# A hybrid attention layer on one core: the inverse softmax sums are turned on VectorE before they are stored

## What is computed

```python
p = softmax(s)                      # per query and head: exp(s - max) / sum
o = einsum(p, v)                    # A, B and M alike; B adds exp(sink - max) to the sum
y = concat([o_a, o_b, o_m], -1) * silu(gate)
x = x + einsum('btm,md->btd', y, w_out)
```

## Time and profile before

| | |
|---|---|
| median of three runs | 1607.84 us |
| lowest and highest | 1602.36, 1608.74 us |
| the profiled execution's own time | 1599.02 us |
| its span, first to last instruction | 1597.2 us |
| PE busy | 1400.2 us, 88% of the span |
| DVE busy | 920.6 us, 58% |
| ACT busy | 657.4 us, 41% |
| POOL busy | 155.9 us, 10% |
| mean granted TensorE clock | 0.949 of full speed |

### The profile page before, as it was taken

How to read it: one execution, slowest core, us unless ns; L and a number is a source line. 1 busy time by engine, 2 the same in 40 slices (tenths; PEclk the granted TensorE clock), 3 DMA queues, 4 the chain that set the end, 5 groups by cost and what they waited for, 6 DMA issues and landing times. The chain is left out here.

```text
span 1597.2 us, 19488 instructions
## 1 busy us (share of the span) xinstructions
PE 1400.2 (88%) x6364; PEld 778.1 (49%) x6364; DVE 920.6 (58%) x2527; ACT 657.4 (41%) x1667; POOL 155.9 (10%) x187
## 2 busy tenths in 40 slices
PE   5988799999889999988599887999997999998881
PEld 3444356666545444444344343666664444544450
DVE  1444636887656677655133446488775557676533
ACT  1123526776634433333111334377655333344332
POOL 1100013300001000000011001132000001000003
PEclk9999999999989999999689998999998999999976
DMA  6100410123132312111241004003124222111106
GB/s 200 53 25 21 156 47 1 45 88 94 67 88 73 80 53 54 26 35 29 62 160 52 25 18 161 27 0 119 35 86 133 54 57 57 54 47 53 34 4 247
DMA packets 117960, 108.58 MB, mean 68 GB/s; under 512 B 52368, under 2 KB 90992, under 8 KB 117872
## 3 DMA queue, kind: packets, MB, share of 16 engines
q1 hardware_dynamic: 117872, 107.45, 22.1%
HBM read 81.76 MB, written 25.76 MB: 67 GB/s over the span
## 5 line engine op out<-in xcount | busy, mean ns | idle before, releaser
L746 PE MATMUL score_ps<-w_slot,hT 128*128 128x512 f32 (+2 forms) x1024 | 391.9, 542 | 12.5 <-ACT prob_bm L1053 7.6
L746 PEld LDWEIGHTS score_ps<-w_slot,hT 128*128 128x128 f32 x1024 | 197.7, 196 | 193.3 <-issue 187.3
L746 PE MATMUL score_ps<-w_slot,work 128*128 128x512 f32 x512 | 234.6, 612 | 5.5 <-issue 5.4
L1099 ACT ACTIVATE hT<-hT,neg_top 128x128 f32<-128x128 f32 (+8 forms) x144 | 116.8, 812 | 288.0 <-DVE neg_top L1372 287.8
L1253 DVE TENSOR_SCALAR_CACHE_REDUCE work<-bias,trial 128x384 f32<-128x384 f32 (+3 forms) x256 | 226.1, 883 | 6.9
L969 ACT ACTIVATE work<-bias,neg_trial 128x768 bf16<-128x768 f32 (+2 forms) x192 | 198.4, 1043 | 67.3 <-DVE neg_trial L1249 67.3
L746 PEld LDWEIGHTS score_ps<-w_slot,work 128*128 128x128 f32 x512 | 97.5, 196 | 129.8 <-issue 129.6
L817 PE MATMUL score_ps<-hT,w_slot 128*128 128x352 f32 x448 | 135.2, 460 | 1.4 <-ACT gate_raw L1083 1.4
L731 PE MATMUL turn_ps<-ident,hT 128*128 128x128 f32 (+1 forms) x720 | 98.9, 277 | 27.6 <-ACT work L1124 17.2
L1154 POOL TENSOR_TENSOR work<-work,norm_sb 128x512 f32<-128x512 f32 (+1 forms) x32 | 38.9, 1216 | 855.7 <-DMA norm_sb<-norm_scratch 855.7
L871 PE MATMUL score_ps<-akT,query_mem 64*128 64x512 f32 (+4 forms) x448 | 103.1, 547 | 9.4 <-ACT prob_bm L1113 6.5
(11 more groups left out here) (179 smaller groups left out, 1768.2 us busy)
## 6 DMA issues: line engine op xcount, KB each, us to landing
w_slot<-in_w_in_dram SPq DMA_DIRECT2D x8, 2048.0 KB, 10.3
gate_raw<-in_x_prompt_dram SPq DMA_DIRECT2D x16, 512.0 KB, 3.7
work<-gate_scratch SPq DMA_DIRECT2D x16, 512.0 KB, 4.7
x_scratch<-gate_raw SPq DMA_DIRECT2D x16, 512.0 KB, 4.6
gate_raw<-x_scratch SPq DMA_DIRECT2D x16, 512.0 KB, 3.5
norm_sb<-norm_scratch SPq DMA_DIRECT2D x56, 128.0 KB, 4.1
gate_scratch<-gate_raw SPq DMA_DIRECT2D x16, 264.0 KB, 3.1
gate_scratch<-gate_raw SPq DMA_DIRECT2D x8, 528.0 KB, 2.6
```

What stands on the lines that cost most here:

```text
L746: last = nc.tensor.matmul(out[:, 0:cols], lhs(k), w[:, k, 0:cols], start=(k == 0), stop=(k == KD - 1))
L1099: ins = nc.scalar.activation(p, p, ACT.Exp, bias=neg, scale=SM_SCALE, accum_out=sums[t % 2][0:r, col:col + 1])
```

## The change

`inv_sum` becomes 32 columns wide, with columns 16 to 31 zeroed once at the start of the program. SCALE makes DVE wait for its reciprocal (`link`), then transposes the tile's `inv_sum` in blocks of 32 by 32 into a new buffer `inv_turned`, of which there is one for each of a and bm and for each of two tiles. In that buffer the eight inverse sums of 32 queries lie on eight partitions, 32 elements each, one such block for every 32 partitions. DVE waits for the transposition too (`signal`), which now gives `inv_made`. `norm_turn` issues four DMAs where it issued one (one for the tile of 32 queries), each of eight rows of 128 bytes. The loads, GATE_SCALE and MIX are the same; the counts that wait for `norm_written` follow the new number of DMAs.

```diff
+def norm_writes(t):
+    return sum(-(-ROWS[n] // 32) for n in range(1, t + 1))
...
-        inv_sum = [sb(f"inv_sum{b}", [P, 16]) for b in range(2)]
+        inv_sum = [sb(f"inv_sum{b}", [P, 32]) for b in range(2)]
+        inv_turned = [[sb(f"inv_turned{b}_{bm}", [P, 32]) for bm in range(2)] for b in range(2)]
...
+                for b in range(2):
+                    nc.gpsimd.memset(inv_sum[b][:, :], 0.0)
...
                         sp.wait_ge(inv_made[bm], t)
-                        with nc.allow_non_contiguous_dma("a head's sums lie one to a partition"):
-                            sp.dma_start(rows.rearrange("c q -> q c"), inv_sum[t % 2][0:r, 8 * bm:8 * bm + 8]
+                        for q in range(0, r, 32):
+                            sp.dma_start(rows[:, q:q + 32], inv_turned[t % 2][bm][q + 8 * bm:q + 8 * bm + 8, :]
                                          ).then_inc(norm_written[bm], 16)
-                        sp.wait_ge(norm_written[bm], 16 * t)
+                        sp.wait_ge(norm_written[bm], 16 * norm_writes(t))
...
                             if t >= 3:
-                                dve.wait_ge(norm_written[bm], 16 * (t - 2))
+                                dve.wait_ge(norm_written[bm], 16 * norm_writes(t - 2))
                             at = slice(8 * bm, 8 * bm + 8)
-                            nc.vector.reciprocal(inv_sum[b][0:r, at], sums[b][0:r, at]).then_inc(inv_made[bm], 1)
+                            link(nc.vector.reciprocal(inv_sum[b][0:r, at], sums[b][0:r, at]))
+                            signal(nc.vector.transpose(inv_turned[b][bm][0:r, :], inv_sum[b][0:r, :]), inv_made[bm], t)
```

## The result

The changed kernel takes 1613.60 us (median of 6 runs, 1611.96 to 1615.43) against 1606.16 us for the kernel before beside it: a ratio of 1.0047, 95% interval [1.0034, 1.0060]. It is 7.4 us slower, and the interval excludes no change. The number lies in the range, but the forecast, nothing on the path, was wrong.

The account below looks back on a forecast made before the run. PE was taken to set the pace in the attention stages. With 0 gained and 0 lost the profiled execution stays at 1599.0 us, 8.8 under the runs' median of 1607.84, so the forecast was 1607, range 1598 to 1617.

Parts of the forecast that it names:

- nothing on the path: Whole kernel: no part of the change gains or loses time, median 1607 us; chance 0.80.
- The store gets shorter: SP's store of the inverse sums: 4.2 us (3.1 to 6.7) for 9.0, about 4.8 less, which nobody waits for.
- the first rival's condition: Slower by stores: four DMAs land one after another, 17.2 us; decides once the store takes 1.85 us longer; 1631, chance 0.06.
- On the path: 0: Attention stages: the shorter store, and separately the longer SCALE on DVE, were each taken to change the kernel's time by 0.
- DVE gets more to do: SCALE in attention grows by 0.35 us (0.28 to 0.55), 32 times, 11 us of DVE work, hidden behind PE.
- T: Time of one added DVE transposition in SCALE, taken as 0.22 us, between bounds of 0.15 and 0.42.
- The cover in front of ADD: DVE's idle time while PE does OUT: at least 0.40 us, 0.72 before PE moves, enough for the longer SCALE.
- the 6 to 13 given as a sign of being right: DVE's busy time would rise by 6 to 13 us if the prediction was right.
- Faster, through the memory system: Rival: single-element stores disturb other traffic or PE's clock; 0.3 us for each of 32 stores, 9.6 back: 1598, chance 0.09.
- The change touches only the attention stages, so I read those first: Opening step: only the two attention stages, 335 and 340 us, were read for what bounds the kernel.
- The sum: All parts together: 0 gained, 0 lost, the profiled execution stays at 1599.0 us.
- What would upset all of it: Something neither queue nor wait shows: a change of PE's granted clock in the attention stages; no size given.

Follow-up runs that it names:

- layer0_straddles: The kernel before with 30 small VectorE instructions more at the start of layer 0, nothing turned: 1620.09 us, 1.0075 times before.
- before_shift: The kernel before with 16 small VectorE instructions more at the start of layer 1, nothing turned: 1617.27 us, 1.0060 times before.

## Why the prediction was wrong

- *The store gets shorter.* Right, and mis-sized: 2.22 us with the issue where 4.2 were taken (3.1 to 6.7), and 28.1 us of SP's standing where some 90 were. The four DMAs neither wait for each other nor land as slowly as single elements do, so the first rival's condition never held.
- *On the path: 0* for the store. Right: MIX and ADD are released by PE as before, and the two kernels with turned stores and the loop elsewhere stand at 1.0008 and 1.0001.
- *DVE gets more to do.* Right: T was taken as 0.22 us and is 0.21 (32 in all, 6.7 us); SCALE grew by 0.36. The cover in front of ADD swallowed it: ADD's waits for PE fell from 118.1 to 106.4 us. VectorE's busy time rose by 17.3 us, above the 6 to 13 given as a sign of being right; 8.0 of them lie in layer 1's search.
- *Faster, through the memory system.* Not seen: packets under 512 B fell by more than half (52368 to 24017), and the kernels with turned stores and the loop elsewhere are not faster than before.
- **The failed step** is in the first sentence: "The change touches only the attention stages, so I read those first". It touches VectorE's program, which holds a loop behind the added instructions. The sum priced what the 32 transpositions do and not that 16 of them stand ahead of layer 1's loop and move it. The missing term is what this set off: 30 ways back of 0.14 us more, which PE's slack would have taken, and the meeting with GpSimd's rope, in all 7.4 us. That the measured time still lies in the range is luck: the range was made from the spread of the runs, not from this.
- *What would upset all of it*, something that neither queue nor wait shows, was also not it: the waits show it, in the row of `trial` behind `bit`, in a stage that I had not listed. That row of before would have given the warning: VectorE waits there for itself, 60 times, 23.2 us, in a stage in which PE had 1.0 of 76.9 us open.

What stays open: why the way back costs 0.51 to 0.63 us at these places, whether the change has a part in the falls of the clock at tiles 7 and 8, and the part of the total of layer0_straddles that its searches do not hold.

## What to carry to other kernels

Instructions added to an engine move all that follows in its program: when a change adds some ahead of a loop, compare the gap in front of the loop's first instruction, before and after, in every loop of that engine, and move the loop by a few idle instructions before blaming the change. A slack is to be read against what runs beside it: twice 0.14 us fitted into the 0.52 us that a pair of steps had, and still 7 us were lost, because the shift brought small instructions under another engine's long ones, and the phase then held itself. A chain that is hidden by 1.8 us is worth nothing when it gets shorter and nearly everything when it gets longer, so both directions are read from the margin, each with all that stands on the same queue.

## What the runs showed of the hardware

- The way back of the same 27-instruction loop on VectorE costs 0.39 us or 0.51 to 0.63 us, by where in the program it lies; the dear places found are 1024 instructions apart. The Trainium skill ("Runtime: NRT & Kernel Launch", Instruction fetch mechanics) says that programs are fetched in blocks of 256 instructions, that a crossing is mostly hidden, and that a branch stalls when its target lies outside the two blocks held. The distance of four blocks agrees; that a loop over a single boundary pays in every step does not follow from it, and the runs show it. The trace shows no fetch for each time round: the instruction queue's packets (number, MB, share) in before_shift, which straddles, are 37, as many as before:

```profile
q14 instruction: 37, 0.30, 0.1%
```

- Of VectorE's instructions beside GpSimd's rope, the small two-input ones (`found`, `trial`, `margin`) and one-input ones (`bit`, `neg_trial`) end with GpSimd's instruction, at 0.56 to 1.28 us for 0.17; the counts, TENSOR_SCALAR_CACHE_REDUCE, keep their 0.60 us beside it.
- Four stores of eight rows of 128 bytes, issued in 1.34 us, had landed 2.2 us after the first issue began; one store of the same 4 KB in single elements took 9.0.
